# A long fp32 model kernel: RWKV's bonus summed by head rows and turned over, stick exponents from running sums of softplus, window weights copied ahead of a gate's low part, and two stage seams re-arranged

## The reference

```python
# rwkv: a sum of 64 products for each of 16 heads and each token
bonus = jnp.sum(heads(r) * heads(k) * r_k, axis=-1, keepdims=True)
y = y + (bonus * heads(v)).reshape(B, T, C)
# mix2, stick-breaking attention, 8 heads, 2 blocks of 128 queries
z = jnp.einsum('bhqd,bkhd->bhqk', q_blk, k) * (dh ** -0.5)
before = key_pos[None, :] < q_pos[:, None]
log_beta = jax.nn.log_sigmoid(z)
log_keep = jnp.where(before, jax.nn.log_sigmoid(-z), 0.0)
suffix = lax.cumsum(log_keep, axis=3, reverse=True) - log_keep
weights = jnp.where(before, jnp.exp(log_beta + suffix), 0.0)
# mix2, sliding windows, 8 heads: softmax over scores and one sink per head
probs = jax.nn.softmax(jnp.concatenate([logits, sink], axis=-1), axis=-1)[..., :-1]
```

## Time and profile before

| what | value |
|---|---|
| median of 3 runs | 2002.63 us |
| the profiled execution's own time | 2002.45 us |
| its span, first to last instruction | 2001.2 us |
| PE busy | 1962.9 us, 98% |
| DVE, ACT, POOL busy | 1477.5, 1093.5, 165.5 us |
| mean granted TensorE clock | 0.996 |
| read from HBM | 349.82 MB, 175 GB/s |

### The profile page before, as it was taken

The page is one execution under the profiler, slowest core; times in us unless marked ns, Lnnn a source line. Parts: engine busy times, 40 slices in busy tenths (PEclk is TensorE's granted clock), DMA queues, the critical chain, the costliest instruction groups (busy, mean ns, idle before and its releaser), DMA issues.

```text
span 2001.2 us, 33195 instructions
## 1 busy us (share of the span) xinstructions
PE 1962.9 (98%) x13160; PEld 1782.8 (89%) x13160; DVE 1477.5 (74%) x2520; ACT 1093.5 (55%) x1680; POOL 165.5 (8%) x93
## 2 busy tenths in 40 slices
PE   8999999999999999899999999999999999999999
PEld 7998889989888998689989778999999999888888
DVE  5775995777667775877757876999999986655555
ACT  5654733366555664766645665545555445555554
POOL 0000013300011000210001003332000000000000
PEclk9999998999999999999999999999999999999999
DMA  6667422266655666246666335555544556666664
GB/s 206 197 208 215 149 79 91 64 189 200 206 188 182 199 198 196 101 143 204 201 206 210 128 120 193 179 183 198 186 163 163 165 174 198 205 203 201 204 205 158
DMA packets 98169, 353.03 MB, mean 176 GB/s; under 512 B 10976, under 2 KB 12896, under 8 KB 97504
## 3 DMA queue, kind: packets, MB, share of 16 engines
q1 hardware_dynamic: 98016, 350.91, 53.9%
HBM read 349.82 MB, written 1.05 MB: 175 GB/s over the span
## 4 chain that ended last, share of the span: by engine, by line
PE 89%; DVE 7%; ACT 2%; issue 1%; POOL 1%; DMA 0%; SPq 0%; ACTq 0%; DVEq 0%
PE psum L317 19%; PE psum L319 18%; PE psum L318 18%; PE psum L331 15%; PE psum L332 8%; DVE tile_low L224 2%; PE psum L2899 2%; PE psum L1162 2%; PE psum L962 1%; PE psum L1042 1%; PE psum L423 1%; POOL small L1809 1%; ACT hT L556 0%; ACT tile_high L212 0%; ACT unread L551 0%
## 5 line engine op out<-in xcount | busy, mean ns | idle before, releaser
L224 DVE TENSOR_TENSOR tile_low<-raw_tiles,tile_high 128x1024 fp32r<-128x1024 f32 x607 | 744.2, 1229 | 331.8 <-ACT tile_high L212 331.2
L212 ACT ACTIVATE tile_high<-raw_tiles 128x1024 fp32r<-128x1024 f32 x642 | 675.6, 1054 | 436.1 <-PE psum L319 432.0
L331 PE MATMUL psum<-hT,tile_high 128*128 128x512 f32 x1408 | 464.1, 384 | 1.9 <-DVE hT L569 1.9
L332 PE MATMUL psum<-hT,tile_low 128*128 128x256 f32 x1408 | 384.1, 273 | 0.0
L317 PE MATMUL psum<-hT,tile_high 128*128 128x256 f32 x1152 | 323.6, 281 | 0.7 <-DVE tile_low L224 0.7
L318 PE MATMUL psum<-hT,tile_high 128*128 128x256 f32 x1152 | 316.8, 275 | 0.0
L319 PE MATMUL psum<-hT,tile_low 128*128 128x256 f32 x1152 | 316.8, 275 | 0.0
L317 PE MATMUL psum<-tile_high,hT 128*128 128x512 f32 (+1 forms) x816 | 311.4, 382 | 4.2 <-DVE tile_low L224 2.5
L318 PE MATMUL psum<-tile_low,hT 128*128 128x512 f32 (+1 forms) x816 | 307.6, 377 | 0.0
L319 PE MATMUL psum<-tile_high,hT 128*128 128x512 f32 (+1 forms) x816 | 307.6, 377 | 0.0
L331 PEld LDWEIGHTS psum<-hT,tile_high 128*128 128x128 f32 x1408 | 266.6, 189 | 39.2 <-DVE hT L569 2.1
(11 more groups left out here) (368 smaller groups left out, 2461.3 us busy)
## 6 DMA issues: line engine op xcount, KB each, us to landing
raw_tiles<-ffn_in_dram SPq DMA_DIRECT2D x176, 512.0 KB, 4.2
raw_tiles<-peer_u_dram SPq DMA_DIRECT2D x128, 512.0 KB, 3.3
raw_tiles<-peer_v_dram SPq DMA_DIRECT2D x128, 512.0 KB, 4.2
raw_tiles<-ffn_out_dram SPq DMA_DIRECT2D x88, 512.0 KB, 4.3
raw_tiles<-w_kv_dram SPq DMA_DIRECT2D x16, 512.0 KB, 4.2
raw_tiles<-in_gates_dram SPq DMA_DIRECT2D x16, 512.0 KB, 3.4
raw_tiles<-peer_q_dram SPq DMA_DIRECT2D x16, 512.0 KB, 3.9
raw_tiles<-w_k_dram SPq DMA_DIRECT2D x8, 512.0 KB, 4.2
```

The lines of the kernel that those rows point to most:

```text
L212: scalar.activation(k.high[:, n % SLOTS, :], k.raw[:, n % RAW_SLOTS, :], ACT.Copy).then_inc(*k.tile_high_made.mark(n))
L224: vector.tensor_tensor(k.low[:, n % SLOTS, :], k.raw[:, n % RAW_SLOTS, :], k.high[:, n % SLOTS, :].bitcast(F32), ALU.subtract).then_inc(*k ...
L331: k.tensor.matmul(both_sums, high[:, c, :], both, start=(c == 0), stop=(c == KC - 1), skip_group_check=True)
L332: ins = k.tensor.matmul(both_sums[:, 0], low[:, c, :], both[:, 0], start=False, stop=(c == KC - 1), skip_group_check=True)
```

## The change

1. **Bonus.** 8 matmuls instead of 16: the selector is now the weight (32 columns of it for a chunk, `sel_and_next`), r times k moves through in 256 columns, and four chunks go to four groups of 32 PSUM partitions. Heads end in the partitions. ACT copies the 128x256 sums into `u(0)` (behind the first group's two value copies); after the second tile of the second group TensorE transposes them in two (`tensor_turn_bonus`), and DVE adds four quarters with one reduction where it had a copy.
2. **Sticks.** With s = softplus(z) = max(z, 0) + log(1 + exp(-|z|)), the log weight is z minus the sum of s from the key to the last one. DVE makes s (one instruction), scans it backwards (two, over a reversed view), subtracts once. ACT needs no bias and does both heads at once.
3. **Windows.** The maximum is taken negated and compared with negated sinks (made once), which removes one 128x2 instruction per window; `turned` moves from the start of step n + 4 to step n + 3, ahead of that step's low part.
4. **Seams.** `in_q_a`'s second tile gets its low part from POOL; `ffn11` starts its sums in banks 6, 7 instead of 4, 5; `vector_kv` makes one low part between the two scalings.

```diff
-SECOND_TILES = [FIRST[name][0] + 1 for name in ("ffn01", "w_kv", "ffn10", "diff_w_q", "diff_w_o", "ffn11", "peer_q")]
+SECOND_TILES = [FIRST[name][0] + 1 for name in ("ffn01", "w_kv", "ffn10", "diff_w_q", "diff_w_o", "ffn11", "in_q_a", "peer_q")]
...
+FFN_BANKS = (((4, 5), (6, 7)), ((6, 7), (4, 5)))
...
-    use_banks(k, range(4, 8))
+    first_sums, next_sums = FFN_BANKS[s == "ffn11"]
+    use_banks(k, first_sums + next_sums)
...
-            use_banks(k, (7,))
+            use_banks(k, next_sums[1:])
             tensor_spread_root(k, s, r["ones"][:, :], r["diagonal"][:, :])
-            use_banks(k, (6, 7, 4, 5))
+            use_banks(k, next_sums + first_sums)
...
             ins.then_inc(*k.tile_used.mark(n))
+            if (g, c0) == (1, 2):
+                tensor_turn_bonus(k)
...
-    for tb in range(TB):
-        for c in range(KC):
-            ins = tensor.matmul(ps[:, tb * HEADS:(tb + 1) * HEADS], r["rk"][:, c, block(tb)], r["sel"][:, c, :],
-                                start=(c == 0), stop=(c == KC - 1))
+    for n in range(2):
+        for quarter in range(QUARTERS):
+            c = 2 * quarter + n
+            ins = tensor.matmul(ps[rows_of(quarter), 0:T], r["sel_and_next"](c), r["rk"][:, c, :],
+                                start=(n == 0), stop=(n == 1))
+    ins.then_inc(*k.bonus_done.mark("bonus"))
+
+
+def tensor_turn_bonus(k):
+    tensor, r = k.tensor, k.room["rwkv"]
+    ps = result(k, "bonus")
+    tensor.wait_ge(*k.v_out.at("bonus"))
+    for tb in range(TB):
+        ins = tensor.transpose(ps[:, (TB + tb) * P:(TB + tb + 1) * P], r["bonus_sums"][:, block(tb)], k.ident)
+    ins.then_inc(*k.bonus_done.mark("turned"))
...
-    vector.wait_ge(*k.bonus_done.at("bonus"))
-    vector.tensor_copy(r["bonus"], result(k, "bonus")[:, 0:TB * HEADS]).then_inc(*k.scaled.mark("bonus"))
+    vector.wait_ge(*k.bonus_done.at("turned"))
+    vector.tensor_reduce(r["bonus"].rearrange("p (b h) -> p b h", b=TB), result(k, "bonus")[:, T:2 * T].rearrange(
+        "p (b q d h) -> p b d h q", b=TB, q=QUARTERS, h=HEADS)[:, :, 0], AX.X, ALU.add).then_inc(*k.scaled.mark("bonus"))
...
         if g == 0:
+            scalar.wait_ge(*k.bonus_done.at("bonus"))
+            scalar.activation(r["bonus_sums"], result(k, "bonus")[:, 0:T], ACT.Copy).then_inc(*k.v_out.mark("bonus"))
             scalar.wait_ge(*k.small_turned.at("TI"))
...
             vector_scale_heads(k, r["piece"](tb, g), r["ss"](tb, g), k.keys_root, (tb, g), k.keys_normed)
+            if tb == 0:
+                split_low(k, first + 4 * g + 5 + SLOTS)
...
-        for h in range(2):
-            ins = scalar.activation(lb[:, h, :], lb[:, h, :], ACT.Exp, bias=pre[:, h, keys - 1:keys])
-        ins.then_inc(*k.stick_made.mark(n))
+        scalar.activation(lb, lb, ACT.Exp).then_inc(*k.stick_made.mark(n))
...
-        vector.tensor_reduce(st[:, 0:2], s, AX.X, ALU.max).then_inc(*done.mark())
+        vector.tensor_reduce(st[:, 0:2], s, AX.X, ALU.max, negate=True).then_inc(*done.mark())
         vector.wait_ge(*done.now())
-        vector.tensor_tensor(st[:, 0:2], st[:, 0:2], sink, ALU.max).then_inc(*done.mark())
+        vector.tensor_tensor(st[:, 0:2], st[:, 0:2], r["neg_sinks"][:, 2 * c:2 * c + 2], ALU.min).then_inc(*done.mark())
         vector.wait_ge(*done.now())
-        vector.tensor_tensor(st[:, 2:4], sink, st[:, 0:2], ALU.subtract)
-        vector.tensor_scalar(st[:, 0:2], st[:, 0:2], -1.0, None, ALU.mult).then_inc(*done.mark((2, n, "top")))
+        vector.tensor_tensor(st[:, 2:4], sink, st[:, 0:2], ALU.add).then_inc(*done.mark((2, n, "top")))
...
-        vector.scalar_tensor_tensor(out=lb, in0=z, scalar=0.0, in1=e, op0=ALU.min, op1=ALU.subtract).then_inc(*done.mark())
-        vector.wait_ge(*done.now())
-
-        vector.tensor_tensor(keep, lb, z, ALU.subtract).then_inc(*done.mark())
+        vector.scalar_tensor_tensor(out=e, in0=z, scalar=0.0, in1=e, op0=ALU.max, op1=ALU.add).then_inc(*done.mark())
         vector.wait_ge(*done.now())
         for h in range(2):
-            ins = vector.tensor_tensor_scan(pre[:, h, :], keep[:, h, :], keep[:, h, :], 0.0, ALU.add, ALU.bypass)
+            back = e[:, h, ::-1]
+            ins = vector.tensor_tensor_scan(passed_on[:, h, ::-1], back, back, 0.0, ALU.add, ALU.bypass)
         ins.then_inc(*done.mark())
         vector.wait_ge(*done.now())
-        vector.tensor_tensor(lb, lb, pre, ALU.subtract).then_inc(*done.mark(n))
+        vector.tensor_tensor(lb, z, passed_on, ALU.subtract).then_inc(*done.mark(n))
...
-            if late == 4 and not stick:
-                turned(n)
...
+        if 0 <= step - 3 < units and not MIX2_UNITS[step - 3][2]:
+            turned(step - 3)
         split = step - 1 if step <= 3 else step
```

More of the change, by code:

```diff
@@ L780, in rwkv_rooms @@
         mid=k.small[:, 16:32], first=k.small[:, 200:216], end=k.small[:, 32:48], carry_scale=k.small[:, 48:56], stats=k.small[:, 64:128],
-        bonus=k.small[:, 128:160], one_less_k_a=k.small[:, 160:168],
+        bonus=k.small[:, 128:160], bonus_sums=u(0)[:, 0:T], one_less_k_a=k.small[:, 160:168],
         v_mean=k.small[:, 168:184], s_mean=k.small[:, 184:200])
+    r["sel_and_next"] = lambda c: masks[:, 2 * P + c * HEADS:2 * P + c * HEADS + SMALL]
     r["b_s"], r["a_s"], r["k_s"], r["r_s"] = r["aT"], r["kk"], r["kT"], r["rT"]
@@ L974, in tensor_bonus @@
     tensor.wait_ge(*k.key_norm.at("bonus_sel"))
+    for n in range(2):
[8 more added lines that the diff above has]
+    tensor.wait_ge(*k.v_out.at("bonus"))
     for tb in range(TB):
-        for c in range(KC):
-            ins = tensor.matmul(ps[:, tb * HEADS:(tb + 1) * HEADS], r["rk"][:, c, block(tb)], r["sel"][:, c, :],
-                                start=(c == 0), stop=(c == KC - 1))
-    ins.then_inc(*k.bonus_done.mark("bonus"))
+        ins = tensor.transpose(ps[:, (TB + tb) * P:(TB + tb + 1) * P], r["bonus_sums"][:, block(tb)], k.ident)
+    ins.then_inc(*k.bonus_done.mark("turned"))
 def tensor_scan_tokens(k):
@@ L2294, in mix2_rooms @@
     m = r["masks"]
-    r.update(window=m[:, 0:3 * P], before=m[:, 3 * P:6 * P], before_neg=m[:, 6 * P:9 * P], bias=u(0), sinks=k.small[:, 16:24],
+    r.update(window=m[:, 0:3 * P], before=m[:, 3 * P:6 * P], before_neg=m[:, 6 * P:9 * P], bias=u(0), sinks=k.small[:, 16:24], neg_sinks=k.small[:, 24:32],
              ones=u(9)[:, 0:P], diagonal=u(9)[:, P:P + T], root=u(9)[:, P + T:P + 2 * T], q_a=tm(u(1))[:, :, 0:BANK],
@@ L2512, in weigh_stick @@
     def weigh_stick(n):
-        pre, lb = mix2_area(k, n, 1), mix2_area(k, n, 2)
-        keys = (MIX2_UNITS[n][1] + 1) * P
+        lb = mix2_area(k, n, 2)
         scalar.wait_ge(*k.stick_steps.at(n))
-        for h in range(2):
-            ins = scalar.activation(lb[:, h, :], lb[:, h, :], ACT.Exp, bias=pre[:, h, keys - 1:keys])
-        ins.then_inc(*k.stick_made.mark(n))
+        scalar.activation(lb, lb, ACT.Exp).then_inc(*k.stick_made.mark(n))
     def turned(n):
@@ L2635, in vector_mix2 @@
     vector.wait_ge(*k.loaded["masks2"].at("all"))
+    vector.tensor_scalar(r["neg_sinks"], r["sinks"], -1.0, None, ALU.mult).then_inc(*k.window_made.mark("sinks"))
+    vector.wait_ge(*k.window_made.at("sinks"))
     def scored_window(n):
@@ L2677, in weigh_stick @@
         c, qb, stick = MIX2_UNITS[n]
-        z, e, lb, keep = (mix2_area(k, n, j) for j in range(4))
-        pre, done = e, k.stick_steps
+        z, e, lb, passed_on = (mix2_area(k, n, j) for j in range(4))
+        done = k.stick_steps
         vector.wait_ge(*k.stick_logs.at(n))
-        vector.scalar_tensor_tensor(out=lb, in0=z, scalar=0.0, in1=e, op0=ALU.min, op1=ALU.subtract).then_inc(*done.mark())
-        vector.wait_ge(*done.now())
-        vector.tensor_tensor(keep, lb, z, ALU.subtract).then_inc(*done.mark())
+        vector.scalar_tensor_tensor(out=e, in0=z, scalar=0.0, in1=e, op0=ALU.max, op1=ALU.add).then_inc(*done.mark())
         vector.wait_ge(*done.now())
         for h in range(2):
-            ins = vector.tensor_tensor_scan(pre[:, h, :], keep[:, h, :], keep[:, h, :], 0.0, ALU.add, ALU.bypass)
+            back = e[:, h, ::-1]
+            ins = vector.tensor_tensor_scan(passed_on[:, h, ::-1], back, back, 0.0, ALU.add, ALU.bypass)
         ins.then_inc(*done.mark())
         vector.wait_ge(*done.now())
-        vector.tensor_tensor(lb, lb, pre, ALU.subtract).then_inc(*done.mark(n))
+        vector.tensor_tensor(lb, z, passed_on, ALU.subtract).then_inc(*done.mark(n))
     def turned(n):
```

## The result

The changed kernel takes 1986.72 us (median of 4 runs, 1986.06 to 1987.21), the kernel before 2002.08 beside it (4 runs, 1998.17 to 2003.36). The ratio is 0.9922, with a 95% interval of 0.991 to 0.9934: 15.4 us faster, between 13 and 18. The forecast was 12.5 faster, 1990.1, and the result stands just inside the lower edge of its range, 1986.5. The direction was right and the size too small by 3 us.

What follows compares the result with a forecast made beforehand. TensorE was taken to bound the kernel, busy 1962.9 of 2001.2 us. The terms -2.1 - 1.6 - 1.2 - 1.25 - 1.65 - 4.7 = -12.5 gave 1989.95, forecast as 1990.1 us; range 1986.5 to 1996.7.

Steps and rivals of the forecast that it cites:

- the attention: Attention of `mix2`: less DVE work and an earlier window copy leave about 1.7 of 6.37 us idle; -4.7 us.
- the clock behind the bonus: Behind the bonus's narrow matmuls: 3.3 us at half clock disappears with them; -1.6 us, bounds 0 and 1.65.
- `kv`: Eighth and twelfth tiles of `kv`: the earlier low part removes two waits of 0.6 us each; -1.2 us.
- a shorter stretch in the scan: Scan: the half-clock stretch comes out 1.65 us shorter, giving 1988.4 us; one part of the range's lower edge.
- all idle time of the attention gone: Attention of `mix2`: the upper bound of its gain, 6.4 us; the other part of the range's lower edge.
- What bounds it: Whole kernel: a microsecond counts only as TensorE's own work, its clock, or a gap before its matmuls; TensorE busy 1962.9 us.
- The bonus's own work: Bonus: 3.49 us of narrow matmuls become 1.07 us of wide ones plus 0.34 for two transposes; -2.1 us.
- The seams: Seams into `ffn11` and `mix2`: free banks and a low part on POOL shorten waits; -1.25 and -1.65 us.
- Rival 1: Scan's half-clock stretch 1.65 us longer or shorter, or the bonus's fall stays: about 1991.7 (1988.4 if shorter); chance 0.17.
- Rivals 2 and 3: Attention of `mix2`: backward scans dearer, 1994 (chance 0.10), or so dear the kernel slows, 2013.9 (0.04 including mishaps).
- Rival 4: Attention of `mix2`: the stick's chain, not DVE's load, sets the pace; half is won, 1992.5; chance 0.14.

Runs made afterwards that it cites:

- e1: The changed kernel with the old bonus of 16-column matmuls put back: 1993.09 us.
- e5: The changed kernel with the old bonus's 32 narrow passes added, sums unused, ahead of the two new transposes: 1990.47 us.
- e8: The changed kernel with its sixteen scans over views in forward order: 1985.8 us.
- e7: The changed kernel with the old stick and window arithmetic, window copies kept in their new place: 1990.18 us.
- e9: The changed kernel again without edit, for another trace and more runs: 1986.15 us.
- e2: The changed kernel with the whole attention of `mix2` as before: 1992.04 us.
- e11: The changed kernel with the new arithmetic, but the copy of turned window weights behind the low part as before: 1989.95 us.
- e13: The kernel before without edit, a third trace: 2002.15 us in one run.

## Why the prediction fell short

Three terms were too small, and they make up 2.45 of the 2.9 us that are missing: the attention (5.85 measured, 4.7 forecast), the clock behind the bonus (2.55, 1.6) and `kv` (1.55, 1.2). Two have one cause, a wait priced at little more than its idle time. That the result still lies inside the range is luck: the edge of 1986.5 was reached by a shorter stretch in the scan and by all idle time of the attention gone, and neither came; by the forecast's own terms these two give 1990.1 - 1.65 - 1.7 = 1986.75.

- **What bounds it**: right. Each us came from TensorE's own work, its clock, or a gap ahead of it.
- **The bonus's own work, 2.1**: 5.5 less the 3.4 lost to the clock in e1, 3.85 less 1.7 in the first pair of traces: 2.1. Right.
- **The clock behind the bonus, 1.6**: right mechanism, size off. e5 showed that the fall goes where the narrow matmuls go, which is also the direction of the rule of the Trainium skill that the forecast named ("TensorE: Matmul & The Clock Gate", "What's actually happening"). But the step "I take the full 1.6; the bounds are 0 and 1.65" took one execution's stretch for the cost. Six traces give one stretch three times and two three times, 2.55 on average and up to 3.4. The bound of 1.65 was wrong.
- **`kv`, 1.2**: 1.55 measured. Each wait costs 0.77, not 0.6: the forecast counted the idle time and the slower first matmul, and left out the 0.16 by which the matmul ahead of the gap is no longer overlapped.
- **The seams, 1.25 and 1.65**: 1.26 to 1.27 and 1.7 measured. The seams of the same kind elsewhere in the trace were good models, to 0.05 us.
- **The attention, 4.7**: 5.85 measured. The idle time went down by 4.8 us (7.1 to 2.3), which is what was forecast. The step that failed is "Of 6.37 us idle about 1.7 remain; -4.7": it took idle time as the whole price. 1.07 us more went, since ten gaps became five and TensorE's matmuls at each gap take some 0.2 us longer. The `kv` part had added 0.1 for the first matmul behind a gap; here nothing was added.
- **Rival 1** (the scan's clock gets 1.65 longer or shorter, or the fall behind the bonus stays): the fall behind the bonus never stayed. The scan's did get longer in three of eight traces with the new bonus, by one piece or two; in both traces of the changed kernel it did not. Whether the new bonus has a part in this stays open. Its price of 1.65 for a stretch was too high for this place, where one more cost 0.4 to 0.5 and two 1.7 to 1.8. **Rivals 2 and 3** (backward scans): fallen by e8. **Rival 4** (the stick's chain sets the pace, and half is won): its mechanism is real, e7 shows waits of 1.5 us for the exponent with the old arithmetic, but the new arithmetic shortens that chain too.

The terms that don't vary add up to 2.1 + 1.55 + 1.27 + 1.7 + 5.85 = 12.5 us. The clock behind the bonus gives 2.55 more: 15.0 us. Over the whole traces the clock's loss differs by 8.95 - 6.4 = 2.55 too, but by the prices above that this agrees is in part luck. From the first sums of `ffn00` to its last matmul TensorE takes 1982.9 us on average in the four traces of the kernel before and 1967.8 in the four with the whole change, 15.1 less. The medians differ by 15.4 in the first session and by 15.8 between e9 and the kernel before beside it. The 0.4 to 0.8 us between are inside the interval of the ratio (13 to 18 us), and I have no cause for them that a trace shows.

## What to carry to other kernels

Price a wait at its idle time plus what the matmuls on both sides of the gap lose, here 0.2 to 0.3 us more for each gap. Read the granted clock in more than one execution before a low stretch goes into a sum: it comes or doesn't come, in whole pieces, and what a piece costs hangs on the work that lies under it. When two results of one engine are asked for in a row, changing their order mostly moves the wait (it won 1.4 of 5.85 us here); order and less work have to come together.

## What the runs showed of the hardware

- Half clock came in pieces: losses of 1.7, 3.4, 5.1, 6.8 and 8.5 us, all multiples of 1.7, in stretches of some 3.4 us each. Behind the same instructions the number of pieces differed from run to run (one or two behind the bonus, none to two in `diff`, three to five in the scan).
- At half clock 16 matmuls of 128x64 took 3.67 us in place of 2.00, and 64 passes of 32x32 took 2.00 in place of 1.98: the small ones don't feel the clock.
- 3.5 us of 16-column matmuls brought a fall in all seven traces that have them, 1.85 us of them in one trace none.
- The clock also fell behind gaps: in e2 and e11 behind a wait of 1.5 us, in e13 behind one of 1.89 us, in e1 behind two of 0.86 and 0.70 us in `mix2`. In the other traces with the same waits it did not, so a gap makes a fall possible, not certain; that the gap is its cause is argued.
- A tensor_tensor_scan over a view with a step of -1 runs as fast as forward, 544 to 545 ns for the mean of both tile sizes.
- DVE's low part of 128x1024 runs at 1.21 us beside POOL's roots of 128x8; a low part of this size on POOL takes 2.38 us.
